# A causal mask moved from VectorE into a TensorE matmul, with a reordered schedule around it, in a hybrid attention block

## What is computed

```python
h    = rms_norm(x, norm_in_w)
proj = h @ w_in                                # a_q a_k a_v a_g b_cq b_ckv b_kr b_g
# mixer A: 16 heads of 64, 2 kv heads, rotary, window of 2 chunks of 64, a sink logit per head
out_a = swa_sink_attention(rope(a_q), rope(a_k), a_v, sinks) * silu(a_g)
# mixer B: 8 heads, low-rank q and kv
q = rms_norm(b_cq) @ w_q_b ;  kv = rms_norm(b_ckv) @ w_kv_b
s = (q_nope @ k_nope.T + q_rope @ k_rope.T) * (128 + 64) ** -0.5
allowed = k_chunk[None, :] <= q_chunk[:, None]   # chunk = token // 64
p = softmax(where(allowed, s, -1e30))
out_b = (p @ v) * silu(b_g)
y = rms_norm(x + concat(out_a, out_b) @ w_out, final_norm_w)
```

## Time and profile before

| | us |
|---|---|
| median of three runs | 680.41 |
| the profiled execution, time | 680.3 |
| its span | 678.5 |
| busy: TensorE matmuls | 669.2 |
| busy: TensorE weight loads | 559.8 |
| busy: VectorE | 338.9 |
| busy: ScalarE | 305.4 |
| busy: GpSimd | 303.1 |
| TensorE's granted clock, mean | 0.997 of full speed |

### The profile page before, as it was taken

How to read it: one execution, slowest core, us unless ns; L and a number is a source line. 1 busy time by engine, 2 the same in 40 slices (tenths; PEclk the granted TensorE clock), 3 DMA queues, 4 the chain that set the end, 5 groups by cost and what they waited for, 6 DMA issues and landing times.

```text
span 678.5 us, 8917 instructions
## 1 busy us (share of the span) xinstructions
PE 669.2 (99%) x3196; PEld 559.8 (83%) x3196; DVE 338.9 (50%) x600; ACT 305.4 (45%) x574; POOL 303.1 (45%) x145
## 2 busy tenths in 40 slices
PE   9999999999999999999999999999999999999995
PEld 8888888888888888888888888888888888888884
DVE  5857132989784645645545578778651100101013
ACT  7723231321343664564465476666754321312233
POOL 0044443354253432532443445556866584464720
PEclk9999999999999999999999999999999999999998
DMA  8632322223222212222321412102124733223215
GB/s 320 233 118 93 111 96 94 91 95 102 84 94 94 93 63 94 93 68 90 101 85 63 155 61 97 63 31 95 32 89 173 290 115 108 93 93 99 88 60 219
DMA packets 21877, 73.54 MB, mean 108 GB/s; under 512 B 2384, under 2 KB 2640, under 8 KB 21712
## 3 DMA queue, kind: packets, MB, share of 16 engines
q1 hardware_dynamic: 18144, 65.61, 28.6%
q10 hardware_dynamic: 3696, 7.43, 3.0%
HBM read 68.83 MB, written 4.19 MB: 108 GB/s over the span
## 4 chain that ended last, share of the span: by engine, by line
PE 93%; DVE 3%; ACT 1%; issue 1%; DMA 1%; DVEq 0%; SPq 0%; ACTq 0%
PE bank L1082 29%; PE bank L1078 29%; PE bank L1081 28%; PE bank L1210 1%; PE bank L1220 1%; PE bank L1329 1%; DMA xs<-x_t 1%; PE bank L1313 1%; PE bank L1232 1%; PE bank L1233 1%; DVE ptb_lo L956 1%; DVE bank L942 1%; PE bank L1101 1%; PE bank L1098 1%; PE bank L1314 0%
## 5 line engine op out<-in xcount | busy, mean ns | idle before, releaser
L283 POOL TENSOR_TENSOR w_lo<-w_raw,w_hi 128x1024 fp32r<-128x1024 f32 x100 | 243.1, 2436 | 317.4 <-ACT w_hi L364 317.4
L364 ACT ACTIVATE w_hi<-w_raw 128x1024 fp32r<-128x1024 f32 x110 | 116.2, 1056 | 208.5 <-PE bank L1078 175.3
L1078 PE MATMUL bank<-x_hi,w_hi 128*128 128x512 f32 x504 | 196.9, 391 | 0.0
L1082 PE MATMUL bank<-x_lo,w_hi 128*128 128x512 f32 x504 | 196.7, 390 | 0.0
L1081 PE MATMUL bank<-x_hi,w_lo 128*128 128x512 f32 x504 | 196.2, 389 | 0.0
L1082 PEld LDWEIGHTS bank<-x_lo,w_hi 128*128 128x128 f32 x504 | 94.6, 188 | 20.1
L1078 PEld LDWEIGHTS bank<-x_hi,w_hi 128*128 128x128 f32 x504 | 94.7, 188 | 18.8 <-DVE mixed L892 0.5
L1081 PEld LDWEIGHTS bank<-x_hi,w_lo 128*128 128x128 f32 x504 | 94.7, 188 | 18.6
L1078 PE MATMUL bank<-w_hi,mx_hi 128*128 128x512 f32 x256 | 100.5, 393 | 0.0
L1081 PE MATMUL bank<-w_hi,mx_lo 128*128 128x512 f32 x256 | 100.0, 391 | 0.0
L1082 PE MATMUL bank<-w_lo,mx_hi 128*128 128x512 f32 x256 | 99.8, 390 | 0.0
(11 more groups left out here) (209 smaller groups left out, 928.9 us busy)
## 6 DMA issues: line engine op xcount, KB each, us to landing
w_raw<-w_stream SPq DMA_DIRECT2D x110, 512.0 KB, 3.3
y<-x_nat ACTq DMA_DIRECT2D x4, 1024.0 KB, 10.5
out<-y SPq DMA_DIRECT2D x6, 512.0 KB, 3.1
xs<-x_t SPq DMA_DIRECT2D x4, 512.0 KB, 5.2
mixed<-x_t SPq DMA_DIRECT2D x4, 512.0 KB, 5.1
fw<-final_w ACTq DMA_DIRECT2D x1, 1024.0 KB, 18.7
cos_b<-tables ACTq DMA_DIRECT2D x2, 256.0 KB, 2.8
sin_b<-tables ACTq DMA_DIRECT2D x2, 256.0 KB, 3.1
```

Source lines behind the costliest of these rows:

```text
L283: pool.tensor_tensor(w_lo[:, s % HL, :], w_raw[:, s % RAW, :], w_hi[:, s % HL, :].bitcast(F32), ALU.subtract)\
L364: act.activation(w_hi[:, s % HL, :], w_raw[:, s % RAW, :], ACT.Copy).then_inc(w_hi_ready, 1)
L1078: ins = pe.matmul(dst, ah, bh, start=start, stop=False)
L1082: return pe.matmul(dst, ah, bl, start=False, stop=stop)
```

## The change

The mask of mixer B is no longer added by VectorE. `b_score` gets a sixth matmul: an identity in bfloat16 (`ident_bf`) as weights and a 128x64 bfloat16 tile `mask_bf` (-1e30 in its first 64 rows, 0 in the others) as the moving operand, added to the last 64 columns of the block. `b_maxima` becomes a plain `reduce_max` with negated result, which does not write the scores back, and the scale of `b_expo` becomes 1. The new constants have places of their own and are set at the kernel's start, so the two memsets at the head of mixer B go. `ones` and `fold` no longer share with a mask.

With it, tables are edited: the half steps of mixer A in t = 0, one entry pair of `LATENT_LOW_AT`, chunks of pairs 0 and 3 in `B_CHUNKS`, `B_ROTARY`, `M_AT`, and the two table loads of pair 0 move from f = 2 to f = 1. The whole diff:

```diff
--- before.py
+++ after.py
@@ -59,11 +59,11 @@
 A_QUADS, A_CHUNKS = 4, SEQ // CHUNK
 
 
-AT_SCORES = [{2: 0, 5: 1, 8: 2, 11: 3}] * 4
-AT_TRANSPOSE = [{5: 0, 8: 1, 11: 2, 14: 3}] * 4
-AT_PV = [{7: 0, 10: 1, 13: 2, 16: 3}] * 4
+AT_SCORES = [{4: 0, 7: 1, 9: 2, 12: 3}] + [{2: 0, 5: 1, 8: 2, 11: 3}] * 3
+AT_TRANSPOSE = [{7: 0, 9: 1, 12: 2, 14: 3}] + [{5: 0, 8: 1, 11: 2, 14: 3}] * 3
+AT_PV = [{9: 0, 11: 1, 14: 2, 16: 3}] + [{7: 0, 10: 1, 13: 2, 16: 3}] * 3
 Q_SPLIT_AT, GATED_AT = 13, 1
-LATENT_AT, LATENT_LOW_AT = {9: 0, 10: 1, 12: 2, 13: 3}, {10: (0,), 11: (1,), 13: (2, 3)}
+LATENT_AT, LATENT_LOW_AT = {9: 0, 10: 1, 12: 2, 13: 3}, {9: (0,), 10: (1,), 13: (2, 3)}
 
 
 
@@ -80,17 +80,17 @@
 
 
 B_SPLITS, B_OWN_SPLITS = {4: 5, 5: 0, 6: 6, 8: 3}, [{0: (1,), 1: (2,)}, {0: (1,), 1: (2,)}, {0: (1,), 1: (2,)}, {0: (1, 2)}]
-B_CHUNKS = [{2: (5,), 4: (6,), 10: (7,)}, {1: (8,), 3: (9,), 10: (10,)}, {1: (11,), 3: (12,), 10: (13,)},
-            {1: (14,), 4: (15,), 6: (16,), 8: (17,), 10: (18,)}]
-
-
-B_ROTARY = [{3: (0,), 4: (1, 2), 5: (3,), 6: (4,), 7: (5,)}] + [{2: (0,), 3: (1,), 4: (2, 3), 5: (4,), 6: (5,)}] * 3
+B_CHUNKS = [{1: (5,), 3: (6,), 10: (7,)}, {1: (8,), 3: (9,), 10: (10,)}, {1: (11,), 3: (12,), 10: (13,)},
+            {1: (14,), 2: (15,), 4: (16,), 7: (17,), 9: (18,)}]
+
+
+B_ROTARY = [{3: (0, 1), 4: (2,), 5: (3,), 6: (4,), 7: (5,)}] + [{2: (0, 1), 3: (2,), 4: (3,), 5: (4,), 6: (5,)}] * 3
 B_ROTARY_FIRST, B_ROTARY_SECOND, B_ROTARY_HIGH = 8, 1, (0, 1, 1, 0)
 B_TAKE = (9, 7, 7, 7)
 
 
 T_BANK = (6, 6, 7, 6, 6, 6, 5, 6)
-M_AT = {3: 2, 5: 3, 7: 4, 9: 5, 10: 6}
+M_AT = {2: 2, 4: 3, 5: 4, 7: 5, 9: 6}
 OUT_PIECES = [2, 1, 1, 1, 1, 1, 2, 2, 2, 1, 2]
 
 
@@ -141,13 +141,13 @@
         eps = at("eps", [P, 1], F32, region(4))
         preloaded = at("preloaded", [P, 1], F32, region(4))
         ident = at("ident", [P, P], F32, region(512))
-        r_consts = region(1024)
-        ones = at("ones", [P, P], F32, r_consts)
-        fold = at("fold", [P, P], F32, r_consts + 512)
-        mask_b = at("mask_b", [P, SEQ], BF16, r_consts)
+        ones = at("ones", [P, P], F32, region(512))
+        fold = at("fold", [P, P], F32, region(512))
         r_sums = region(512)
         ones_r = at("ones_r", [P, P], F32R, r_sums)
         fold_r = at("fold_r", [P, P], F32R, r_sums)
+        ident_bf = at("ident_bf", [P, P], BF16, region(256))
+        mask_bf = at("mask_bf", [P, CHUNK], BF16, region(128))
         st_a = at("st_a", [P, 2, 6, 4], F32, region(192))
         st_b = at("st_b", [P, 4, 4], F32, region(64))
         sumsq = at("sumsq", [P, TOK, 4], F32, region(64))
@@ -240,7 +240,7 @@
         gate_silu, gated = sem("gate_silu"), sem("gated")
         cqs_split, b_hi, b_lo = sem("cqs_split"), sem("b_hi"), sem("b_lo")
         b_rot_evac, b_rot, b_rot_hi, b_rot_lo = sem("b_rot_evac"), sem("b_rot"), sem("b_rot_hi"), sem("b_rot_lo")
-        b_mask, b_scores, b_max, b_exp, b_recip, b_probs = sem("b_mask"), sem("b_scores"), sem("b_max"), sem("b_exp"), sem("b_recip"), sem("b_probs")
+        b_scores, b_max, b_exp, b_recip, b_probs = sem("b_scores"), sem("b_max"), sem("b_exp"), sem("b_recip"), sem("b_probs")
         b_turned, b_pt_hi, b_pt_lo, b_pv, b_out = sem("b_turned"), sem("b_pt_hi"), sem("b_pt_lo"), sem("b_pv"), sem("b_out")
         m_hi, m_lo, m_lo_pool = sem("m_hi"), sem("m_lo"), sem("m_lo_pool")
         o_done, o_evac, o_squared, o_gained, o_sum, o_total, o_root = sem("o_done"), sem("o_evac"), sem("o_squared"), sem("o_gained"), sem("o_sum"), sem("o_total"), sem("o_root")
@@ -523,7 +523,7 @@
                 u = w % 8
                 n = P * (u % 4 + 1)
                 act.wait_ge(b_max, w + 1)
-                act.activation(B[4 + u % 2][:, 0:n], B[4 + u % 2][:, 0:n], ACT.Exp, bias=st_b[:, u % 4, 0:1], scale=-1.0,
+                act.activation(B[4 + u % 2][:, 0:n], B[4 + u % 2][:, 0:n], ACT.Exp, bias=st_b[:, u % 4, 0:1],
                                accum_out=st_b[:, u % 4, 2:3]).then_inc(b_exp, 1)
 
             def b_pt_high(w):
@@ -570,7 +570,8 @@
                     elif step[0] == "T":
                         b_pt_high(w)
                     elif step[0] == "F":
-                        if p == 0 and f == 2:
+                        if p == 0 and f == 1:
+
                             act.wait_ge(gated, 8)
                             act.dma_start(cos_b[1][:, :], tables[:, P:P + SEQ]).then_inc(rot_landed, 16)
                             act.dma_start(sin_b[1][:, :], tables[:, P + SEQ:P + 2 * SEQ]).then_inc(rot_landed, 16)
@@ -647,7 +648,10 @@
         def _(dve):
             dve.memset(eps[:, :], EPS).then_inc(consts_set, 1)
             dve.memset(ones[:, :], 1.0).then_inc(consts_set, 1)
+            dve.memset(mask_bf[:, :], 0.0).then_inc(consts_set, 1)
+            dve.wait_ge(consts_set, 3)
             dve.memset(v_t[:, 0:CHUNK], 0.0)
+            dve.memset(mask_bf[0:64, :], MASK_VALUE).then_inc(consts_set, 1)
             dve.sem_inc(a_pt_lo, 1)
             dve.sem_inc(a_out, 1)
             dve.sem_inc(b_pt_lo, 1)
@@ -681,6 +685,7 @@
                     x_sum(j - 1)
             x_sum(7)
             dve.wait_ge(tables_landed, 48)
+            dve.tensor_copy(ident_bf[:, :], ident[:, :]).then_inc(consts_set, 1)
             dve.wait_ge(x_summed, 7)
             dve.tensor_copy(ones_r[:, :], ones[:, :])
 
@@ -699,7 +704,7 @@
 
             dve.tensor_tensor(cos_r[:, :], cos_r[:, :], rstd[:, :], ALU.mult)
             dve.tensor_tensor(sin_r[:, :], sin_r[:, :], rstd[:, :], ALU.mult).then_inc(consts_set, 1)
-            dve.wait_ge(consts_set, 4)
+            dve.wait_ge(consts_set, 7)
 
             def rotate_terms(src, cos, sin, count, evac=proj_evac):
 
@@ -936,10 +941,7 @@
                 u = w % 8
                 n = P * (u % 4 + 1)
                 dve.wait_ge(b_scores, w + 1)
-
-
-                sc = B[4 + u % 2][:, 0:n]
-                dve.tensor_tensor_reduce(sc, sc, mask_b[:, SEQ - n:], -1.0, 3e38, ALU.add, ALU.min, st_b[:, u % 4, 0:1]).then_inc(b_max, 1)
+                dve.reduce_max(st_b[:, u % 4, 0:1], B[4 + u % 2][:, 0:n], AX.X, negate=True).then_inc(b_max, 1)
 
             def b_normalise(w):
                 u = w % 8
@@ -961,13 +963,8 @@
                 m = mixed[:, A_TILES + head, :]
                 dve.tensor_tensor(m, B[7][:, :], m, ALU.mult).then_inc(b_out, 1)
 
-
-            dve.memset(mask_b[:, :], 0.0).then_inc(b_mask, 1)
-            dve.wait_ge(b_mask, 1)
-            dve.memset(mask_b[0:CHUNK, SEQ - CHUNK:], MASK_VALUE).then_inc(b_mask, 1)
             for part in range(6):
                 b_rotary(0, part)
-            dve.wait_ge(b_mask, 2)
             b_tile_low(5)
             b_rotary_low(0, 0)
             b_tile_low(0)
@@ -1233,6 +1230,7 @@
                     ins = pe.matmul(B[7][:, of_chunk], v, pta_lo[:, of_chunk], start=False, stop=c == 1)
                 ins.then_inc(a_pv, 1)
 
+            pe.wait_ge(consts_set, 6)
             for t in range(4):
                 for hf in range(16):
                     if hf in AT_PV[t]:
@@ -1312,7 +1310,9 @@
                 q = slice(P * i, P * i + P)
                 pe.matmul(dst, qr[par][:, h, q], kr_hi[:, 0:n], start=True, stop=False)
                 pe.matmul(dst, qr[par][:, h, q], kr_lo[:, 0:n], start=False, stop=False)
-                three(dst, qn_hi[par][:, h, q], qn_lo[par][:, h, q], kn_hi[par][:, h, 0:n], kn_lo[par][:, h, 0:n], False, True).then_inc(b_scores, 1)
+                three(dst, qn_hi[par][:, h, q], qn_lo[par][:, h, q], kn_hi[par][:, h, 0:n], kn_lo[par][:, h, 0:n], False, False)
+
+                pe.matmul(B[4 + w % 2][:, n - CHUNK:n], ident_bf[:, :], mask_bf[:, :], start=False, stop=True).then_inc(b_scores, 1)
 
             def b_transpose(w):
                 pe.wait_ge(b_probs, w + 1)
```

## The result

| | before | after |
|---|---|---|
| median | 680.53 | 688.62 |
| lowest and highest | 680.30, 681.02 | 687.51, 689.06 |
| the profiled execution | 680.3 | 688.8 |
| its span | 678.5 | 687.0 |
| mean granted TensorE clock | 0.997 | 0.994 |

A forecast was written before the change was run, and what follows sets the result against it. TensorE was taken to bound the kernel, busy 669.2 of 678.5 us. Masks +3.5, mixer A +0.6, pair 0 +0.4, pair 3 +0.5 and waits that go -1.4 gave +3.6, so 684.0 us; range 681.7 to 686.0.

The forecast's parts named there:

- Mixer A, t = 3: First latent's low part on VectorE ahead of quad 2's normalisation; it just fits: 0, at most 0.2 us.
- The masks: Mixer B: 32 score blocks get one more weight load and 64-column matmul, 0.11 us each, paid in full: +3.5 us.
- Rivals 1 and 4: 1: cheap masks, 0.03 to 0.05 us each, 681.4 to 682.1, chance 0.13. 4: not slower, 679.7, chance 0.06.
- Mixer A, t = 0: Quads 1 and 3 have two half steps from scores to transposes; TensorE waits 0.3 us twice: +0.6 us.
- Pair 0: Mixer B: ScalarE's wait for gates and the issues move to f = 1; transposes T1 wait: +0.4 us.
- Pair 3: Mixer B: ScalarE's split and chunk at f = 2 delay block 3's probabilities; transposes T3 wait: +0.5 us.
- Pairs 0 to 2: Mixer B, rotation: one part instead of two at f = 4; waits before S6 go, -1.2, those at T1 shrink, -0.2.
- Rival 3: Worse convoy: ScalarE's and VectorE's order costs waits counted as 0, or type changes cost more: 685.5 to 686.5, chance 0.12.

The follow-up runs named there:

- the entry: LATENT_LOW_AT's low part of the first latent at half step 9 instead of 10 in t = 3: alone in the kernel before 685.50 us; taken back in the changed kernel 683.60.
- the halves: GpSimd's low part of a chunk as two 512-column instructions: kernel before with the entry 680.59 us; whole changed kernel 685.10; kernel before 679.05.
- the run without it: Changed kernel with the entry taken back and the half steps of mixer A's t = 0 as before: 682.05 us, ratio 1.0025.

## Why the prediction was wrong

- **Mixer A, t = 3** is the step that failed: "The low part of the first latent ... takes 0.7, and the normalisation 1.1 ... It just fits: 0, at most 0.2." It cost 5.3. The instructions' durations were taken as fixed. They are not while GpSimd reads two SBUF inputs beside them: 0.7 became 2.47, and the 0.17 of a 128x4 sum 2.29. Taken alone and taken back, the entry is worth 5.2 and 5.0. A second term hung on it, the 1.6 us of matmuls at 1.2 GHz after the wait. With the halves the wait shrinks to 1.30 and the slow matmuls go.
- **The masks**: 0.11 each was right, 3.5 us in the trace. The forecast had the mask's own load pass beneath the matmul ahead of it; it does not, but starts with its matmul (492.96). Whether the 0.09 beyond the columns is the next load lying open stays open. What was missed is that the stage does not pay them whole: 1.8 us fall into waits that they themselves or VectorE's relief take away. In the sum this was hidden, because I had booked those waits as gained by the rotation's table, which alone costs 1.0 us. Rivals 1 and 4 on a cheap mask hold for a *second* mask (0.03, its columns), not for the first.
- **Mixer A, t = 0**: 0.6 forecast, 1.3 in the trace, 1.5 by the run without it. The waits before the transposes were 0.4 each instead of 0.3; the one around quad 3's product was not seen.
- **Pair 0**: 0.4 forecast, 0.58. **Pair 3**: 0.5 forecast, 0.29; the masks ahead of T3 gave more time. The forecast's own rows give 0.4 there (497.0 less 496.6), not the 0.5 of its sum. **Pairs 0 to 2**: -1.4 forecast, -1.8. The forecast called 1.6 us the most that any relief can give back; it left out that S6's second matmul comes 0.10 late behind each of the three waits.
- **The places of the tiles**: not in the forecast at all, -0.7. Without it the rest of the change would have come to 684.3, as near to 684.0 from the other side. That the change without the latent's entry comes within 0.4 us of the forecast is in part luck: mixer A's t = 0 and pair 0 were 0.9 too low together, and the waits that go, pair 3 and the places 1.3 too high.
- **Rival 3** held such a convoy, but gave t = 3 no more than 0.2, so its upper end was 2 us short. (Its items give 685.4 or 686.1, and 687.5 together, not 685.5 to 686.5.) The bound rested on durations seen with GpSimd idle. The profile of before did hold the warning: the rotation's last instruction (L932) takes 1.75 us in pair 1, and of its eight executions four take 0.69 and four 1.45 to 1.76.

What stays open: why tiles 384 bytes further on make matmuls faster by nanoseconds, and what the 0.09 us is paid for that a mask costs beyond its columns. Neither was tried.

## What to carry to other kernels

Before moving a VectorE instruction with two SBUF inputs, look in GpSimd's timeline at what runs at its new place: its duration is about its own plus the rest of GpSimd's instruction, and a tiny one pays as much as a large one. Look for one line whose instructions differ in duration at equal shape; here that spread was the contention, and it marked both a risk and a gain. And price a table edit only together with what else moves the due times: the masks alone, the rotation alone and the two together each had another set of waits.

## What the runs showed of the hardware

- VectorE with two SBUF inputs stands until GpSimd's running instruction ends: 2.47 and 2.29 us against 2.40 of GpSimd, 1.37 and 1.25 against 1.30. With one input in a bank, VectorE took its usual 0.69 while GpSimd ran (373.11, with the halves). When VectorE is first, GpSimd stands: 3.05 us for two instructions that took 2.55.
- TensorE after a wait of 3.49 us ran some eight matmuls at 1.2 GHz (0.427 us for 512 columns; granted clock 0.63 over that stretch); after 1.30 and 1.33 us none did.
- In a float32 stream a bfloat16 matmul of 64 columns with its load costs 0.12 us (0.075 behind blocks of 128 keys), and a second one right behind it 0.03.
- The same instructions with tiles 384 bytes further on took 0.7 us less of 680.
